# Two-layer trunk on one core: three query products of the second mixer placed among the latent norms and before the last head's rotation

## The chip, the cores and the metric

The kernel runs on one core of a Trainium2 chip. The metric is device time of the whole program in microseconds (us). The kernel before was run three times: 3219.42, 3215.95 and 3207.77 us, median 3215.95 us.

## The reference, cut to what matters

Two layers over 512 positions of width 1024, all in f32. Of one layer:

```
h = rmsnorm(x) * (1 + sc1) + sh1
proj = h @ w_in                      # xa_q 256, xa_kv 160, xb, xc, xd, gates 4*1024
y_a = mla_mixer(xa_q, xa_kv, ...)    # A: latents cq (256) and ckv (128), each with its own rmsnorm,
                                     #    then q = cq @ w_q_up, k and v = ckv @ w_kv_up; rope on 32 of 96 rows
y_b = chunk_relbias_mixer(xb)        # B: q, k, v of 8 heads straight from proj
y_c = diff_mixer(xc)                 # C
y_d = swa_sink_mixer(xd)             # D
merged = sum over the four of sigmoid(gates) * (y @ w_branch)
x = x + g1 * (merged @ w_out)
...                                  # second half: shared expert and 64 routed experts, top 6
```

The six modulations (sc1, sh1, g1, ...) are products of a short vector with `ada_w`, 48 column tiles of 128 for each layer.

## The kernel before

**Products and jobs.** f32 matrix products are done as three products of split operands: a weight tile is split into `w_hi` and `w_lo`, an activation into `h_hi` and `h_lo`, and hi*hi, hi*lo and lo*hi are added in one PSUM bank. The projections of the first half of a layer are written as jobs (`Job`, `make_jobs` L100). A job of the input projection is 8 slices of the contraction times 3, that is 24 products of 128x512 (L690); a job of a branch projection (`o_hi`) is 12, a job of the query latents (`cq_hi`, 96 rows) 6, a job of the key and value latents (`ckv_hi`) 3. Jobs use two PSUM banks in turn, so a job waits until the output of the job two before it has been copied out (by ScalarE, `act_out` from L701, or VectorE, `dve_out`).

**Weights.** SyncE loads weight tiles of 128x1024 (512 KB) into a ring of three buffers `raw` (`load_tile` L593). ScalarE makes `w_hi` (`split_hi`, L616), VectorE `w_lo` (`split_lo`, L624), each into two buffers in turn. A `raw` buffer is loaded again only when both halves of its tile have been split. The split of a tile is an event at the first product of the tile ahead of it in the stream (`events_of`).

**Modulations in the same ring.** The 48 column tiles of `ada_w` that a later stage needs go through the same ring. `place_ada` (L82) hangs them behind jobs: it takes the jobs with weights of projB, gbA, projC, gbB, projD, gbC and gbD, the last job of each phase left out, and sets tile i behind job i * (number of jobs) // 48. VectorE works such a tile off in one pass of 128x1024 (L823) behind the output of the job that it hangs on, and its `raw` buffer is free only then.

**Order on TensorE, by layer.** The order is the order of the code (from L1412). First the spread of the root of the first norm; projA (cq tile 0, cq tile 1, ckv, krope); then for cq and then for ckv the norm: `pe_norm_sums` (L895, column sums of squares with a vector of ones), `dve_norm_mean` (L901), `pool_norm_root` (L906), `pe_norm_spread` (L913, the root spread over a bank), `dve_norm_apply` (L926) and `act_norm_apply` (L944). The squares come from ScalarE (L882) and VectorE (L884). The sums and the spread use the same PSUM bank MB. Then the rotation of the shared key rows (L1422); upA (8 key jobs, 4 value jobs, 8 query jobs, with the rotation of head h-1, L1427, behind the job of head h); and the rotation of the last head. Then attention A (scores L984, transposes L1038, output L1118), in whose 17 steps the 16 jobs of projB are spread as filling (`spread`), and behind it, with no attention beside it, the gate stage gbA: four groups of two gate jobs of 24 products and two branch jobs of 12. Attention B is filled with projC and followed by gbB, attention C is filled with projD, attention D with gbC and followed by gbD. ScalarE and VectorE carry the same order in their own blocks (`act_stream` L794, `dve_stream` L807).

**Memory.** Before, the latents (`cqf`, `ckvf`, their split halves) lie in the area that qB, kB and vB take later.

## Time and profile before

| | |
|---|---|
| runs | 3219.42, 3215.95, 3207.77 us |
| median | 3215.95 us |
| the profiled execution | 3210.36 us, span 3208.7 us |
| TensorE busy | 2916.7 us (91%), 13756 matmuls |
| VectorE busy | 2033.4 us (63%) |
| ScalarE busy | 1568.6 us (49%) |
| GpSimd busy | 611.6 us (19%) |
| mean granted TensorE clock | 0.943 |

The shares are averages over the whole span, and the two layers each have a first half (mixers) and a second half (experts). The change lies in the first halves, at 72 to 770 us in layer 0 and at the same places 1580 us later in layer 1. The granted clock is 1.00 at 2.4 GHz and 0.50 at 1.2 GHz; a value between them is a mean over a stretch.

### The profile page before, as it was taken

To read this page: it belongs to the slowest core of one execution; us is meant where nothing else is said; L and a number is where in the kernel's file an instruction comes from. 1 tells how busy PE (TensorE), PEld (TensorE's weight loads), DVE (VectorE), ACT (ScalarE), POOL (GpSimd) and SP (SyncE) were. 2 spreads that over 40 slices of the span, in tenths; PEclk is the share of its full clock that TensorE was granted. 3 is DMA by queue.
4 is the path that set the end of the run, shared out by engine and by line. 5 is a ranking of instruction groups with operands and counts; after the bars stand their busy time and mean duration, and the time that the engine had idled before them with its cause. 6 is when DMAs were issued, how large, how long until landed. Compare 5 with 4: busy or idle time off the path is not lost. (4 is left out here: it accounts for less than half of the span.)

```text
span 3208.7 us, 42356 instructions
## 1 busy us (share of the span) xinstructions
PE 2916.7 (91%) x13756; PEld 2217.9 (69%) x13756; DVE 2033.4 (63%) x2871; ACT 1568.6 (49%) x2422; POOL 611.6 (19%) x577
## 2 busy tenths in 40 slices
PE   5899998899879999999579999989998899999993
PEld 4577776677667777777456777756776677777773
DVE  4544446454468888888645444555545788888885
ACT  2342423432347777777233334243223677777770
POOL 0100000100133333333210000000003233333332
PEclk9899999999789999999669999999998899999995
DMA  7124332233469999999412243312324799999975
GB/s 227 55 86 144 105 131 79 84 111 119 154 242 362 364 368 370 359 360 351 192 52 73 92 144 111 131 60 86 129 100 192 289 367 358 362 371 365 357 260 207
DMA packets 119333, 671.67 MB, mean 209 GB/s; under 512 B 27468, under 2 KB 28876, under 8 KB 84204
## 3 DMA queue, kind: packets, MB, share of 16 engines
q1 hardware_dynamic: 85792, 605.91, 50.7%
q0 software_dynamic: 31456, 57.70, 5.5%
q10 hardware_dynamic: 1932, 6.16, 0.8%
q8 instruction: 78, 1.28, 0.2%
q14 instruction: 75, 0.61, 0.1%
HBM read 656.86 MB, written 55.02 MB: 222 GB/s over the span
## 5 line engine op out<-in xcount | busy, mean ns | idle before, releaser
L1831 DVE TENSOR_TENSOR ew_lo<-ew,e_hi 128x2048 fp32r<-128x2048 f32 x260 | 595.8, 2292 | 191.9 <-ACT e_hi L1689 191.7
L690 PE MATMUL bank<-h_hi,w_hi 128*128 128x512 f32 x1248 | 514.5, 412 | 50.9 <-DVE w_lo L624 19.3
L1689 ACT ACTIVATE e_hi<-ew 128x2048 fp32r<-128x2048 f32 x260 | 497.5, 1914 | 105.4 <-PE bank L1976 81.5
L624 DVE TENSOR_TENSOR w_lo<-raw,w_hi 128x1024 fp32r<-128x1024 f32 x198 | 242.7, 1226 | 439.4 <-ACT w_hi L616 439.2
L690 PE MATMUL bank<-h_hi,w_lo 128*128 128x512 f32 x1248 | 503.1, 403 | 0.0
L690 PE MATMUL bank<-h_lo,w_hi 128*128 128x512 f32 x1248 | 500.8, 401 | 0.0
L1976 PE MATMUL bank<-e_hi,x_hi 128*128 128x512 f32 x1040 | 419.7, 404 | 0.0
L1976 PE MATMUL bank<-ew_lo,x_hi 128*128 128x512 f32 x1040 | 408.7, 393 | 0.0
L1976 PE MATMUL bank<-e_hi,x_lo 128*128 128x512 f32 x1040 | 406.5, 391 | 0.0
L616 ACT ACTIVATE w_hi<-raw 128x1024 fp32r<-128x1024 f32 x198 | 208.2, 1052 | 283.6 <-DMA raw<-in_wmix 184.3
L1591 POOL DMA_INDIRECT y_d<-y,idx x128 | 219.1, 1712 | 624.1 <-issue 527.0
L690 PEld LDWEIGHTS bank<-h_hi,w_hi 128*128 128x128 f32 x1248 | 240.2, 192 | 136.9 <-issue 47.0
L690 PEld LDWEIGHTS bank<-h_hi,w_lo 128*128 128x128 f32 x1248 | 240.5, 193 | 65.2 <-issue 12.4
L690 PEld LDWEIGHTS bank<-h_lo,w_hi 128*128 128x128 f32 x1248 | 240.7, 193 | 56.9 <-issue 8.7
L1011 ACT ACTIVATE pr<-sn,negmax 128x256 f32<-128x256 f32 (+3 forms) x256 | 137.0, 536 | 227.6 <-DVE negmax L1002 227.3
L1996 PE MATMUL bank<-ew,actT 128*128 128x512 f32 x520 | 247.2, 598 | 0.0
L1557 POOL DMA_INDIRECT xg<-h_d,idx x128 | 193.2, 1509 | 215.4 <-issue 203.3
L1976 PEld LDWEIGHTS bank<-e_hi,x_lo 128*128 128x128 f32 x1040 | 195.9, 188 | 44.1
L1976 PEld LDWEIGHTS bank<-e_hi,x_hi 128*128 128x128 f32 x1040 | 196.6, 189 | 38.5
L1976 PEld LDWEIGHTS bank<-ew_lo,x_hi 128*128 128x128 f32 x1040 | 196.6, 189 | 37.1
L1952 PEld LDWEIGHTS bank<-cst,xg 128*128 128x128 f32 x1040 | 123.8, 144 | 96.1 <-issue 68.7
L1824 DVE TENSOR_TENSOR x_lo<-bank,x_hi 128x512 fp32r<-128x512 f32 x260 | 166.7, 682 | 18.5 <-ACT x_hi L1681 18.5
(289 smaller groups left out, 4454.1 us busy)
## 6 DMA issues: line engine op xcount, KB each, us to landing
ew<-in_wexp SPq DMA_DIRECT2D x130, 2048.0 KB, 9.7
raw<-in_wmix SPq DMA_DIRECT2D x297, 512.0 KB, 4.0
ew<-in_wexp SPq DMA_DIRECT2D x130, 1024.0 KB, 9.4
yt<-y_d SPq DMA_DIRECT2D x8, 3072.0 KB, 15.6
ada0a<-in_ada SPq DMA_DIRECT2D x2, 2048.0 KB, 13.5
ada0b<-in_ada SPq DMA_DIRECT2D x2, 2048.0 KB, 22.3
h_d<-htok ACTq DMA_DIRECT2D x8, 512.0 KB, 2.7
xg<-h_d,idx POOLq DMA_INDIRECT x130, 9.4
```

What stands on the lines that cost most here:

```text
L616: nc.scalar.activation(w_hi[q % SPLIT][:], raw[u % RAW][:], ACT.Copy).then_inc(hi_done, 1)
L624: nc.vector.tensor_tensor(w_lo[q % SPLIT][:], raw[u % RAW][:], w_hi[q % SPLIT][:].bitcast(F32), ALU.subtract).then_inc(lo_done, 1)
L690: ins = nc.tensor.matmul(out, lhs, rhs, start=start, stop=stop)
L1011: nc.scalar.activation(pr[u % 4][:, 0:mp.nk], sn[u % 2][:, 0:mp.nk], ACT.Exp, bias=negmax[:, u:u + 1], scale=-1.0, accum_out=psum_of[:, u: ...
L1557: nc.gpsimd.indirect_dma_start(out=xg[s][0:n, :], out_offset=None, in_=h2_d, in_offset=bass.IndirectOffsetOnAxis(ap=idx[j % 8][0:n, 0:1].b ...
L1591: nc.gpsimd.indirect_dma_start(out=y_d, out_offset=bass.IndirectOffsetOnAxis(ap=idx[j % 8][0:n, 1:2].bitcast(U32), axis=0), in_=y[j % 2][0 ...
L1689: nc.scalar.activation(e_hi[h][:], up_part(ew, j, h), ACT.Copy).then_inc(whi_done, 1)
L1824: nc.vector.tensor_tensor(x_lo[j % 2][:, 4 * b:4 * b + 4, :], TB[b][:].rearrange("p (k t) -> p k t", k=4), x_hi[j % 2][:, 4 * b:4 * b + 4, ...
L1831: nc.vector.tensor_tensor(up_part(ew_lo, j, h), up_part(ew, j, h), e_hi[h][:].bitcast(F32), ALU.subtract).then_inc(wlo_done, 1)
L1952: ins = nc.tensor.transpose(TB[b][:, k * P:(k + 1) * P], xg[s][:, (4 * b + k) * P:(4 * b + k + 1) * P], ident)
L1976: ins = nc.tensor.matmul(G[s % 2][:], a, w, start=(h, k, i) == (0, 0, 0), stop=(h, k, i) == (1, 3, 2))
L1996: ins = nc.tensor.matmul(bank[1][:], actT[s % 2][:, f, :], raw_w[:, f, S:D], start=f == 0, stop=f == 1)
```

## The change

Of the four query jobs of mixer B, two (`early`: query tiles 0 and 1) run among the latent norms and one (`late`: query tile 2) ahead of the last head's rotation; projB keeps query tile 3, the key and value jobs and the turns. The krope job runs behind the sums of cq. The sums of the norms go to the bank OB, cq in columns 0 to 3 and ckv in 4 to 7, and no longer to MB; the spread now waits for MB itself. The latents lie in the gate buffers and in the area of the attention's output, so that qB can be written while they are in use. projB has 13 jobs in place of 16, so that `place_ada` divides 48 tiles over 87 jobs and not 90, and sets them at other jobs.

```diff
--- before.py
+++ after.py
@@ -107,7 +107,10 @@
                 + [Job("VA", [("kvup",)], "vA", act="ckv", k=1, arg=t) for t in range(TC)]
                 + [Job("T", [("qup", h // 4)], "qA", act="cq", k=2, m=DQ, col=DQ * (h % 4), arg=h) for h in range(HA)])
     for br, c in (("B", C_B), ("C", C_C)):
-        j["proj" + br] = ([Job("T", tile(c + P * i), "q" + br, arg=i) for i in range(4)]
+        q = [Job("T", tile(c + P * i), "q" + br, arg=i) for i in range(4)]
+        if br == "B":
+            j["early"], j["late"], q = q[0:2], q[2:3], q[3:]
+        j["proj" + br] = (q
                           + [Job("T", tile(c + P * (4 + i)), "k" + br, arg=i) for i in range(4)]
                           + with_turns([Job("T", tile(c + P * (8 + i)), "vt", arg=4 * (br == "C") + i) for i in range(4)],
                                        [Job("turn", [], "v" + br, arg=i) for i in range(4)]))
@@ -128,7 +131,7 @@
     return j
 
 
-ORDER = ("projA", "upA", "projB", "gbA", "projC", "gbB", "projD", "gbC", "gbD", "out", "shared")
+ORDER = ("projA", "early", "upA", "late", "projB", "gbA", "projC", "gbB", "projD", "gbC", "gbD", "out", "shared")
 
 
 def tile_stream():
@@ -260,12 +263,13 @@
         qB = place("qB", [P, 4, S])
         kB = place("kB", [P, 4, S])
         vB = place("vB", [P, TC, BW])
-        cqf = place("cqf", [P, 2, S], at=r1)
-        ckvf = place("ckvf", [P, 1, S], at=r1 + 4096)
-        cq_hi = place("cq_hi", [P, 2, S], F32R, at=r1 + 6144)
-        cq_lo = place("cq_lo", [P, 2, S], F32R, at=r1 + 10240)
-        ckv_hi = place("ckv_hi", [P, 1, S], F32R, at=r1 + 14336)
-        ckv_lo = place("ckv_lo", [P, 1, S], F32R, at=r1 + 16384)
+        cqf = place("cqf", [P, 2, S], at=t_end["gt0"] - 4 * S)
+        ckvf = place("ckvf", [P, 1, S], at=t_end["o_hi"] - 16 * S)
+        cq_hi = place("cq_hi", [P, 2, S], F32R, at=t_end["ckvf"])
+        cq_lo = place("cq_lo", [P, 2, S], F32R, at=t_end["cq_hi"])
+        ckv_hi = place("ckv_hi", [P, 1, S], F32R, at=t_end["cq_lo"])
+        ckv_lo = place("ckv_lo", [P, 1, S], F32R, at=t_end["ckv_hi"])
+        assert t_end["ckv_lo"] <= t_end["o_lo"] and t_end["cqf"] == t_end["gt1"]
         qC = place("qC", [P, 4, S], at=r0)
         kC = place("kC", [P, 4, S], at=r0 + 8192)
         vC = place("vC", [P, TC, BW], at=r0 + 16384)
@@ -558,7 +562,7 @@
 
 
         m_use = {}
-        for key in ([("st", n) for n in ("x",)] + [("rb", "x"), ("st", "cq"), ("rb", "cq"), ("st", "ckv"), ("rb", "ckv"), ("kr", 0)]
+        for key in ([("st", n) for n in ("x",)] + [("rb", "x"), ("rb", "cq"), ("rb", "ckv"), ("kr", 0)]
                     + [("qr", h) for h in range(HA)] + [("ot", o) for o in range(16)] + [("st", "x2"), ("rb", "x2")]):
             m_use[key] = len(m_use)
 
@@ -584,6 +588,7 @@
         def wait_mb_full(eng, key):
             eng.wait_ge(m_full, m_full_no[key] + 1)
 
+        norm_stats = {"cq": OB[:, 0:TC], "ckv": OB[:, TC:2 * TC], "x2": MB[:, 0:TC]}
         norm_no = {"cq": 0, "ckv": 1, "x2": 2}
         sq_k0 = {"cq": 0, "ckv": 2, "x2": 3}
         norm_k = {"x": KD, "cq": 2, "ckv": 1, "x2": KD}
@@ -886,19 +891,21 @@
 
         def pe_norm_sums(pe, name):
 
-            wait_mb_free(pe, ("st", name))
             K = norm_k[name]
+            stats = norm_stats[name]
+            if ("st", name) in m_use:
+                wait_mb_free(pe, ("st", name))
             for k in range(K):
                 n = sq_k0[name] + k
                 pe.wait_ge(sq_ready[n % 2], n // 2 + 1)
                 for t in range(TC):
-                    ins = nc.tensor.matmul(MB[:, t:t + 1], square_buf(name, n)[:, t * P:(t + 1) * P], ones[:, 0:1],
+                    ins = nc.tensor.matmul(stats[:, t:t + 1], square_buf(name, n)[:, t * P:(t + 1) * P], ones[:, 0:1],
                                            start=(k == 0 and t == 0), stop=(k == K - 1), skip_group_check=True)
                 ins.then_inc(sq_used, 1)
 
         def dve_norm_mean(dve, name):
             dve.wait_ge(sq_used, sq_k0[name] + norm_k[name])
-            nc.vector.tensor_scalar(stat[:, 0:TC], MB[:, 0:TC], 1.0 / (norm_k[name] * P), EPS, ALU.mult,
+            nc.vector.tensor_scalar(stat[:, 0:TC], norm_stats[name][:, 0:TC], 1.0 / (norm_k[name] * P), EPS, ALU.mult,
                                     ALU.add).then_inc(ms_ready, 1)
 
         def pool_norm_root(pool, name):
@@ -909,6 +916,7 @@
 
             if name in norm_no:
                 pe.wait_ge(rstd_ready, norm_no[name] + 1)
+                wait_mb_free(pe, ("rb", name))
             for t in range(TC):
                 ins = nc.tensor.matmul(MB[:, t * P:(t + 1) * P], rstd[:, t:t + 1].broadcast_to([P, P]), ident,
                                        start=True, stop=True)
@@ -1333,12 +1341,14 @@
                     act_norm_apply(act, "x", mod[:, 0:KD], h_hi, [pr[0][:], pr[1][:]])
                     act.wait_ge(lam_ready, 2)
                     nc.scalar.activation(lamt[:, 2:4], lamt[:, 0:2], ACT.Exp).then_inc(lame, 1)
-                    act_stream(act, events_of(whole(jobs["projA"])))
+                    act_stream(act, events_of(whole(jobs["projA"][:3])))
                     norm_squares(act, "cq", cqf, ready=lambda e, k: wait_out_of(e, "cq", k))
+                    norm_squares(act, "ckv", ckvf, ready=lambda e, k: wait_out_of(e, "ckv", 0))
+                    act_stream(act, events_of(whole(jobs["projA"][3:])))
                     act_norm_apply(act, "cq", None, cq_hi, [pr[0][:], pr[1][:]])
-                    norm_squares(act, "ckv", ckvf, ready=lambda e, k: wait_out_of(e, "ckv", 0))
+                    act_stream(act, events_of(whole(jobs["early"][:1])))
                     act_norm_apply(act, "ckv", None, ckv_hi, [pr[0][:], pr[1][:]])
-                    act_stream(act, events_of(whole(jobs["upA"])))
+                    act_stream(act, events_of(whole(jobs["early"][1:] + jobs["upA"] + jobs["late"])))
                     for i, br in enumerate("ABCD"):
                         act_attention(act, br)
                         if br != "C":
@@ -1365,12 +1375,15 @@
                                                              accum_out=lamt[:, i:i + 1]).then_inc(lam_ready, 1)
                     nc.vector.tensor_tensor(lamt[:, 6:7], vec[:, V_SUB:V_SUB + 1], vec[:, V_OML:V_OML + 1], ALU.mult)
                     nc.vector.tensor_scalar(sinkt[:, 0:32], vec[:, V_SINK:V_SINK + 32], -1.0, None, ALU.mult)
-                    dve_stream(dve, events_of(whole(jobs["projA"])))
+                    dve_stream(dve, events_of(whole(jobs["projA"][:3])))
                     norm_squares(dve, "cq", cqf, ready=lambda e, k: wait_out_of(e, "cq", k))
                     dve_norm_mean(dve, "cq")
+                    dve_stream(dve, events_of(whole(jobs["projA"][3:])))
                     dve_norm_apply(dve, "cq", cqf, vec[:, V_GQ:V_GQ + 2], None, cq_hi, cq_lo, [pr[0][:], pr[1][:]])
                     dve_norm_mean(dve, "ckv")
+                    dve_stream(dve, events_of(whole(jobs["early"][:1])))
                     dve_norm_apply(dve, "ckv", ckvf, vec[:, V_GKV:V_GKV + 1], None, ckv_hi, ckv_lo, [pr[0][:], pr[1][:]])
+                    dve_stream(dve, events_of(whole(jobs["early"][1:])))
                     dve.wait_ge(lame, 1)
                     link(dve, nc.vector.tensor_tensor(lamt[:, 4:5], lamt[:, 3:4], lamt[:, 2:3], ALU.subtract))
                     link(dve, nc.vector.tensor_tensor(lamt[:, 5:6], lamt[:, 4:5], vec[:, V_LI:V_LI + 1], ALU.subtract))
@@ -1394,6 +1407,7 @@
                         dve_stream(dve, events_of([(j, 0, n_products(j))]))
                         if j.out == "qA" and j.arg:
                             rotate(j.arg - 1)
+                    dve_stream(dve, events_of(whole(jobs["late"])))
                     rotate(HA - 1)
                     dve.wait_ge(tabA_ready, 1)
                     for i, br in enumerate("ABCD"):
@@ -1412,11 +1426,18 @@
                 @block.tensor
                 def _(pe):
                     pe_norm_spread(pe, "x")
-                    for j in jobs["projA"]:
-                        pe_products(pe, j, 0, n_products(j))
-                    for name in ("cq", "ckv"):
-                        pe_norm_sums(pe, name)
-                        pe_norm_spread(pe, name)
+                    def products_of(js):
+                        for j in js:
+                            pe_products(pe, j, 0, n_products(j))
+
+                    products_of(jobs["projA"][:3])
+                    pe_norm_sums(pe, "cq")
+                    products_of(jobs["projA"][3:])
+                    pe_norm_spread(pe, "cq")
+                    pe_norm_sums(pe, "ckv")
+                    products_of(jobs["early"][:1])
+                    pe_norm_spread(pe, "ckv")
+                    products_of(jobs["early"][1:])
                     wait_out_of(pe, "krope")
                     wait_mb_free(pe, ("kr", 0))
                     nc.tensor.matmul(MB[R, :], prot, qraw[R, :], start=True, stop=True).then_inc(m_full, 1)
@@ -1430,6 +1451,7 @@
                         pe_products(pe, j, 0, n_products(j))
                         if j.out == "qA" and j.arg:
                             rotate(j.arg - 1)
+                    products_of(jobs["late"])
                     rotate(HA - 1)
                     for br in "ABCD":
                         pe_attention(pe, br)
```

The listings below show one engine's instructions in program order: `w_hi_70` is buffer number 70, and so on.

ScalarE around the latent norms of a layer, before:

```order
L715 ACTIVATE ckvf<-bank 128x512
L616 ACTIVATE w_hi_70<-raw_68 128x1024
L882 ACTIVATE sn_74<-cqf 128x512
L944 ACTIVATE cq_hi<-pr_76 128x512
L944 ACTIVATE cq_hi<-pr_77 128x512
L882 ACTIVATE sn_74<-ckvf 128x512
L944 ACTIVATE ckv_hi<-pr_76 128x512
L616 ACTIVATE w_hi_71<-raw_69 128x1024
L717 ACTIVATE kA<-bank 64x512 x8
```

The same place of the change:

```order
L720 ACTIVATE ckvf<-bank 128x512
L887 ACTIVATE sn_74<-cqf 128x512
L887 ACTIVATE sn_74<-ckvf 128x512
L621 ACTIVATE w_hi_70<-raw_68 128x1024
L952 ACTIVATE cq_hi<-pr_76 128x512
L952 ACTIVATE cq_hi<-pr_77 128x512
L621 ACTIVATE w_hi_71<-raw_69 128x1024
L727 ACTIVATE qB<-bank 128x512
L952 ACTIVATE ckv_hi<-pr_76 128x512
L621 ACTIVATE w_hi_70<-raw_67 128x1024
L727 ACTIVATE qB<-bank 128x512
L621 ACTIVATE w_hi_71<-raw_68 128x1024
```

Both squares now stand together ahead of the next weight split, and two copies of query tiles and two splits stand among the applications of the norms (L952) and behind them.

TensorE at the last head's rotation, before (L1427 is a rotation, L984 the scores of attention A):

```order
L690 MATMUL bank<-cq_hi,w_hi_70 96x512
L690 MATMUL bank<-cq_lo,w_hi_70 96x512
L690 MATMUL bank<-cq_hi,w_lo_72 96x512
L1427 MATMUL bank<-qA,cst 32x512 x2
L984 MATMUL bank<-kA,qA 128x128 x2
L984 MATMUL bank<-kA,qA 128x256 x2
L690 MATMUL bank<-h_hi,w_hi_71 128x512
```

The same place of the change:

```order
L695 MATMUL bank<-cq_hi,w_hi_70 96x512
L695 MATMUL bank<-cq_lo,w_hi_70 96x512
L695 MATMUL bank<-cq_hi,w_lo_72 96x512
L1448 MATMUL bank<-qA,cst 32x512
L695 MATMUL bank<-h_hi,w_hi_71 128x512
L695 MATMUL bank<-h_lo,w_hi_71 128x512
L695 MATMUL bank<-h_hi,w_lo_73 128x512
```

The two rotations that stood together are parted by the 24 products of query tile 2, of which the last three rows are the first; the second rotation and the scores follow them.

VectorE at the boundary of the third and the fourth group of the second gate stage gbB (L775 and L778 multiply the gate with the branch and add it to the sum, L823 is a modulation tile, L624 a weight split), before:

```order
L778 TENSOR_TENSOR merged<-merged,gt_84 128x512
L823 ISA raw_68,mod<-raw_68,cb,vec 128x1024
L823 ISA mod 128x1
L624 TENSOR_TENSOR w_lo_73<-raw_67,w_hi_71 128x1024
L624 TENSOR_TENSOR w_lo_72<-raw_69,w_hi_70 128x1024
```

The same place of the change:

```order
L783 TENSOR_TENSOR merged<-merged,gt_84 128x512
L828 ISA raw_67,mod<-raw_67,cb,vec 128x1024
L828 ISA mod 128x1
L629 TENSOR_TENSOR w_lo_73<-raw_67,w_hi_71 128x1024
L828 ISA raw_69,mod<-raw_69,cb,vec 128x1024
```

A second modulation tile now stands behind the first gate job of this group.

## Rows read from the trace of the kernel before

**Rows 1.** Windows: start:end, us, busy PE, PEld, DVE, ACT, POOL, granted clock, DMA share, GB/s.
```profile
78.50:95.70 17.20, 10.06 (x44) 7.61 (x42) 6.13 (x12) 3.36 (x5) 2.04 (x2) 0.56 0.00 2
95.70:107.70 12.00, 12.00 (x37) 7.92 (x36) 5.27 (x7) 4.73 (x8) 6.29 (x5) 0.77 0.21 56
133.20:246.40 113.20, 112.44 (x666) 86.17 (x664) 50.67 (x116) 46.83 (x106) 3.06 (x6) 0.99 0.26 91
246.40:317.10 70.70, 68.39 (x290) 54.93 (x288) 30.18 (x37) 17.73 (x22) 0.00 (x0) 0.98 0.39 138
695.00:769.50 74.50, 67.45 (x290) 53.52 (x288) 34.61 (x45) 22.15 (x29) 0.00 (x0) 1.00 0.40 137
1675.30:1686.40 11.10, 11.10 (x37) 6.93 (x36) 5.27 (x7) 4.74 (x8) 6.29 (x5) 0.87 0.22 61
```

**Rows 2.** Waits of TensorE in attention A (133.2 to 246.4): us, times, longest.
```profile
PE bank L690 <- ACT gt L734: 0.4, 1, 0.4
```

**Rows 3.** Timeline of TensorE, 17 products inside attention A: start us, us busy.
```profile
147.08 0.40 PE L690 MATMUL bank<-h_lo,w_hi 128*128 128x512 f32 x1
...
150.72 0.39 PE L690 MATMUL bank<-h_hi,w_lo 128*128 128x512 f32 x1
```

**Rows 4.** Timeline of TensorE, last two rotations and first scores; [idle before <- releaser].
```profile
126.00 1.04 PE L1427 MATMUL bank<-qA,cst 32*32 32x512 f32 x2
127.91 1.30 PE L1427 MATMUL bank<-qA,cst 32*32 32x512 f32 x2 [0.87 <-DVE qrot L1389]
129.14 1.22 PE L984 MATMUL bank<-kA,qA 96*128 96x128 f32 x4
```

**Rows 5.** Timeline of TensorE, norms of the latents, layer 0.
```profile
72.69 0.39 PE L690 MATMUL bank<-h_hi,w_lo 128*128 128x512 f32 x1
...
78.44 0.95 PE L895 MATMUL bank<-ones,sn 128*128 128x1 f32 x8
80.11 1.34 PE L895 MATMUL bank<-ones,sn 128*128 128x1 f32 x8 [0.72 <-DVE sn L884]
82.83 2.07 PE L913 MATMUL bank<-cst,rstd 128*128 128x128 f32 x8 [1.38 <-POOL rstd L906]
87.68 1.84 PE L895 MATMUL bank<-ones,sn 128*128 128x1 f32 x8 [2.77 <-ACT sn L882]
90.86 2.07 PE L913 MATMUL bank<-cst,rstd 128*128 128x128 f32 x8 [1.34 <-POOL rstd L906]
93.86 1.88 PE L1422 MATMUL bank<-qraw,cst 32*32 32x512 f32 x2 [0.93 <-DVE pr L926]
95.67 0.80 PE L690 MATMUL bank<-ckv_hi,w_hi 128*128 128x512 f32 x1
```

**Rows 6.** Timeline of TensorE, 11 of the first latent products.
```profile
96.27 0.63 PE L690 MATMUL bank<-ckv_lo,w_hi 128*128 128x512 f32 x1
...
100.54 0.63 PE L690 MATMUL bank<-ckv_hi,w_lo 128*128 128x512 f32 x1
```

**Rows 7.** Waits of TensorE in the first gate stage (246.4 to 317.1).
```profile
PE bank L690 <- DVE w_lo L624: 2.3, 1, 2.3
```

**Rows 8.** Timelines of VectorE, ScalarE, TensorE in that stage, one chain.
```profile
263.87 1.28 DVE L823 CUSTOM_DVE_ANT_0 raw<-raw,cb,vec 128x1024 f32<-128x1024 f32 x1
...
268.55 1.06 ACT L616 ACTIVATE w_hi<-raw 128x1024 fp32r<-128x1024 f32 x1 [7.86 <-DMA raw<-in_wmix]
...
269.64 1.23 DVE L624 TENSOR_TENSOR w_lo<-raw,w_hi 128x1024 fp32r<-128x1024 f32 x1 [4.48 <-ACT w_hi L616]
...
271.01 0.47 PE L690 MATMUL bank<-h_hi,w_hi 128*128 128x512 f32 x1 [2.31 <-DVE w_lo L624]
```

**Rows 9.** Waits of TensorE in the second gate stage (427.1 to 497.0).
```profile
PE bank L690 <- DVE w_lo L624: 2.1, 2, 1.9
```

**Rows 10.** Waits of TensorE in the last gate stage (695.0 to 769.5).
```profile
PE bank L690 <- DVE gt L775: 5.4, 3, 2.3
PE bank L690 <- DVE w_lo L624: 1.5, 1, 1.5
```

## Prediction

> **What bounds the kernel now.** I read the views in this order: the share of each engine, to see which is the candidate; then the windows of each stage that the change touches; then in each stage what TensorE waited for; and last the timeline of the two places where work is put in. The kernel as a whole is a TensorE kernel, busy for 91% of the span, but the stages differ. In attention A TensorE is busy for 112.44 of 113.20 us at a clock of 0.99, while VectorE works 50.67 and ScalarE 46.83 [rows 1], and its one listed wait for a copy is 0.4 us [rows 2]. What is taken out there comes off the time one for one. Among the latent norms it is the other way round: TensorE is busy for 10.06 of 17.20 us, and the clock granted there is 0.56 [rows 1]; a chain of small steps over three engines sets the length. In the gate stages TensorE is bound again, but for some stalls on the ring of weight tiles and on VectorE: one of 2.3 us in gbA [rows 7], 2.1 in gbB [rows 9], 5.4 and 1.5 in gbD [rows 10]. So the change takes work from a stage that pays for it in full and puts most of it into a stage with idle time. All terms below are for one layer, and there are two.
>
> **1. Three query tiles leave attention A.** That is 3 x 24 = 72 products. Seventeen of them in a row start from 147.08 to 150.72, 3.64 us over 16 steps, so 0.2275 us each at the full clock [rows 3]. 72 x 0.2275 = 16.4 us. The other engines have room for the shorter steps: VectorE and ScalarE would still be busy for about half of 97 us [rows 1], and they lose copies and splits as well. **-16.4.** If steps of the attention began to wait for the softmax, part of this would stay; with cover of two to one I take the whole.
>
> **2. One query tile before the last rotation.** +24 x 0.2275 = +5.5 us. It stands where the second rotation waited 0.87 us for VectorE to finish the one before [rows 4]; that wait is covered now. **+4.6.** Its split and copy lie on ScalarE and VectorE beside 24 products that hide them. If the last rotation came late behind the split of the next tile on VectorE (1.23 us, [rows 8]), 0.4 more, which I leave out.
>
> **3. The latent norms.** Before, from the end of the products of ckv (72.69 plus 0.39, 73.1) to the first latent product at 95.67 it took 22.6 us [rows 5]. That held the 24 products of krope (5.5 us) and then sums, roots and spreads almost one behind the other. After, the chain on TensorE is: a wait for the copy and the square of the last cq tile, estimated at 1.2 from the two sums of cq (a wait of 0.72 and what the first sum leaves); sums of cq 0.95 + 1.34; krope 5.5, which hides the root; spread 1.0 to 2.07; sums of ckv 0.9 to 1.84; qB0 5.5, which hides the root and the application of cq; spread of ckv 1.0 to 2.07; qB1 5.5, which hides the application of ckv and the split of the latent weights; rotation 1.0 to 1.88. The upper values are the rows' own [rows 5], at a clock near one half; the lower are half of them, for the full clock. The sum is 23.9 to 27.9; I take 25.5, since the stretch now has three blocks of 24 products and should see the full clock for most of it. That is +2.9 for 48 products more, whose bare price is 10.9: the idle time of the norms takes in the rest.
>
> Behind it, the key and value products took 12.00 us at a clock of 0.77 in layer 0 and 11.10 at 0.87 in layer 1 [rows 1]. Eleven products at the low clock, from 96.27 to 100.54 in ten steps, are 0.427 us apart [rows 6], against 0.2275. If TensorE comes out of qB1 at the full clock, 36 products cost about 10, so 1 to 2 us come back; I take 1.5. Together **+1.4**, bounds -1 and +5.
>
> **4. The modulation tiles move.** With 87 jobs and not 90, projB loses two tiles (7 to 5), gbA and gbB each gain one (8 to 9), and in all gate stages they hang on other jobs. What such a tile costs is one chain [rows 8]: VectorE ends it at 265.15 (263.87 + 1.28), its buffer is loaded and the split begins at 268.55, 3.4 us later, the low half begins at 269.64, and the first product runs at 271.01, 5.86 us after the tile was done. A job of 24 products covers 5.5, so when the tile hangs on the second branch job and a second one on the next gate job, the following gate job stalls: 2.31 here. In gbA the new list has no such place but two groups that look like the groups of gbD, which stalls on VectorE's sum three times for 5.4 in all [rows 10]; since in gbA that sum is one pass, not two, I take 1 (0 to 4.6, gbD's 6.9 less the 2.3 it has). In gbB the last group has just that place, with one VectorE pass more ahead of it (estimate 2.3 + 0.7 to 1.2, so 3.5), and two boundaries like those of gbD that cost 2.3 and less, 3.1 together: 6.6 for 2.1 now, +4.5. In gbC and gbD one of the boundaries goes: -1.5. Sum **+4**, bounds -1 and +7. Attention B, C and D have the same number of tiles or nearly so, at zero.
>
> **5. Buffers and bank.** The latents in other buffers and the sums in another bank add no instruction. The new bank lets the sums of ckv be written while the spread of cq is still being read; that is in the sum of part 3. Two weight tiles more are needed among the norms; the DMA share there is 0.00 with the ring full [rows 1], so they cost nothing; uncovered, one would cost a load of 3.4 [rows 8].
>
> **Sum.** -16.4 + 4.6 + 1.4 + 4 = -6.4 for a layer, **-12.8** for two. From the profiled execution's 3210.4 that is 3197.6. That execution lies 5.6 below the median of the runs, 3215.95; against the median I forecast **3203 us**.
>
> **The rivals.** (R1) *The gate stages don't pay.* If the moved modulation tiles land in slack, part 4 falls to about -1 to 0 and part 3 to 0, and a layer gains 11 to 13 us: 3190 to 3195 in all. For it: TensorE's stalls in gbA and gbB are few now with nearly as many tiles [rows 7, 9]. Against it: the place that makes a stall of 2.31 is in the new list of gbB once, with more VectorE work ahead of it. Chance 0.30.
>
> (R2) *The moved products are given back almost whole.* Parts 3 and 4 at their bounds (+5 and +7) leave -16.4 + 4.6 + 12 = 0 a layer: 3210 to 3217. For it: gbD, whose pattern gbA and gbB take over, loses 6.9 us to such stalls in one stage [rows 10]. Against it: two bounds at once. Chance 0.15.
>
> (R3, slower) *The clock stays low.* Before, the norm stretch had a mean clock of 0.56 [rows 1] with TensorE busy for over half of it, and the first latent products ran 0.427 apart [rows 6]. If the bursts of 24 products between sums and spreads stay at 1.2 GHz, the 72 products of krope, qB0 and qB1 cost 0.2 us more each, +14.4 a layer, which with R2's part 4 is -6.4 - 4 + 14.4 + 7 = +11, so +22 in all: 3230 to 3240. It decides from some 32 of the 72 products at the low clock, where the gain of 6.4 is gone (6.4 / 0.2). Against it: in gbD four stalls of up to 2.3 us left the clock at 1.00 [rows 1, 10], and by part 3 no new gap is longer than those. For it: gbA with one such stall shows 0.98, not 1.00 [rows 1, 7]. Chance 0.07. The Trainium skill speaks for this rival (TensorE: Matmul & The Clock Gate, "A second HAM failure mode: psum-queue depth-cycling"): where TensorE idles briefly and often between groups of products, its clock swings between the two rates, and what is lost is the fall and the climb between bursts. By that rule the norm stretch would come out as in R3; gbD's row, four stalls at a clock of 1.00, doesn't bear it out for gaps of this size.
>
> That the change doesn't do what it says I give nothing: the listing shows the 24 products between the rotations. What is left, 0.03, is for things not thought of, on either side.
>
> **How the numbers follow.** The forecast with its own width, 3197 to 3210, has 0.45, R1 0.30, R2 0.15, R3 0.07. The range 3187 to 3214 takes in the forecast, R1 with its lower bounds and more than half of R2, over 0.8. About 0.5%, 16 us, is what a measurement of this kernel can tell from no change, so the border of faster is at 3200. R1 lies below it, and a quarter of the forecast's width: 0.30 + 0.12 = 0.42. Slower begins at 3232: 0.07. The rest is 0.51.
>
> **What would show it.** In the profile after: attention A shorter by 16 us with TensorE still busy for nearly all of it; 24 products between the last two rotations and no wait of 0.87 there; 24 to 28 us from the end of ckv to the first latent product, with a clock well over 0.56 and key and value products in about 10; TensorE's waits for w_lo and gt of 3 to 4 us in gbA, 6 to 7 in gbB, and one less in gbD. The prediction is wrong if attention A doesn't shorten by the full 72 products, if the norm stretch is longer than 28 us or shorter than 23, or if the waits in gbA and gbB stay at 2.3 and 2.1.

## The result and the profile after

The changed kernel takes 3191.03 us (median of 7 runs, 3178.43 to 3195.51). The kernel before has a median of 3209.29 us over seven runs, of which three stand ahead of the prediction with a median of 3215.95; 12.8 less than 3209.29 would have been 3196.5. The ratio is 0.9929 (0.9913 to 0.9945), a gain of 18 to 28 us, 23 in the middle (18 by the two medians). The forecast was 12.8 us less, most likely inside the 0.5% that count as no change; the time of 3191 lies inside the range of 3187 to 3214, but in the part given to the first rival. So the direction was right and the size about half of what came.

The profiled execution took 3187.87 us. Its first lines on the page:

```profile
span 3186.2 us, 42356 instructions
## 1 busy us (share of the span) xinstructions
PE 2903.4 (91%) x13756; PEld 2209.2 (69%) x13756; DVE 2033.6 (64%) x2871; ACT 1569.8 (49%) x2422; POOL 611.7 (19%) x577
```

The instructions are the same in number, so the 22.5 us between the two spans are waits and TensorE's clock (0.949 on the mean, 0.943 before). The windows of the stages after follow, with the columns of [rows 1]; the first is the norm stretch, then the key and value products, attention A, gbA, gbB, attention D with gbC, gbD, all of layer 0, and gbA of layer 1:

```profile
73.60:96.90 23.30, 22.11 (x115) 17.43 (x115) 9.03 (x14) 7.97 (x12) 2.04 (x2) 1.00 0.21 71
96.90:107.00 10.10, 9.96 (x38) 5.95 (x37) 5.31 (x8) 5.39 (x9) 6.29 (x5) 1.00 0.27 70
132.80:234.70 101.90, 98.64 (x602) 74.43 (x601) 47.86 (x116) 43.06 (x104) 3.06 (x6) 0.98 0.23 78
234.70:312.10 77.40, 70.57 (x292) 55.96 (x290) 30.97 (x39) 18.17 (x22) 0.00 (x0) 0.96 0.37 129
421.80:497.60 75.80, 68.86 (x290) 54.70 (x291) 35.85 (x47) 18.28 (x22) 0.00 (x0) 0.98 0.37 132
586.90:689.00 102.10, 100.80 (x586) 75.51 (x585) 59.31 (x144) 42.23 (x111) 5.16 (x11) 0.97 0.32 108
689.00:762.60 73.60, 67.40 (x290) 53.56 (x288) 34.75 (x45) 21.81 (x29) 0.00 (x0) 1.00 0.40 140
...
1801.80:1874.50 72.70, 67.62 (x290) 53.61 (x292) 30.88 (x40) 18.40 (x22) 0.00 (x0) 1.00 0.39 138
```

TensorE among the norms after, with the columns of [rows 5]. What stood in [rows 5] as six small operations with five gaps of 0.7 to 2.8 us is now small operations between blocks of 24 products, and one gap is left, the 1.21 ahead of the first sums. The sums of ckv take 0.95 us where they took 1.84, and a spread takes 1.05 where it took 2.07:

```profile
74.79 1.95 PE L902 MATMUL bank<-ones,sn 128*128 128x1 f32 x16 [1.21 <-ACT sn L887]
82.18 1.06 PE L921 MATMUL bank<-cst,rstd 128*128 128x128 f32 x8
83.07 0.95 PE L902 MATMUL bank<-ones,sn 128*128 128x1 f32 x8
89.45 1.05 PE L921 MATMUL bank<-cst,rstd 128*128 128x128 f32 x8
95.91 1.04 PE L1443 MATMUL bank<-qraw,cst 32*32 32x512 f32 x2
96.88 0.50 PE L695 MATMUL bank<-ckv_hi,w_hi 128*128 128x512 f32 x1
```

And ahead of attention A, with the columns of [rows 4]: query tile 2 fills the place between the last two rotations, and the wait of 0.87 is gone.

```profile
125.21 1.04 PE L1448 MATMUL bank<-qA,cst 32*32 32x512 f32 x2
126.18 0.50 PE L695 MATMUL bank<-h_hi,w_hi 128*128 128x512 f32 x1
...
131.86 1.04 PE L1448 MATMUL bank<-qA,cst 32*32 32x512 f32 x2
132.83 0.71 PE L992 MATMUL bank<-kA,qA 96*128 96x128 f32 x4
```

TensorE's waits in gbA (234.7 to 312.1), gbB (421.8 to 497.6) and gbD (689.0 to 762.6) after, two lines for each, to set beside [rows 7, 9, 10]:

```profile
PE bank L695 <- DVE merged L780: 4.1, 2, 2.1
PE bank L695 <- DVE w_lo L629: 2.7, 2, 2.0
...
PE bank L695 <- DVE w_lo L629: 4.6, 2, 3.3
PE bank L695 <- DVE gt L780: 2.3, 2, 1.6
...
PE bank L695 <- DVE gt L780: 3.9, 2, 2.3
PE bank L695 <- DVE w_lo L629: 2.3, 2, 1.7
```

The stages in us, layer 0 and layer 1, between the two profiles; the forecast is the one for a layer. An attention stage goes from the start of its first to the end of its last instruction on TensorE, and a gate stage is what lies between two of them (gbD ends with its own last product):

| stage | before | after | difference | forecast |
|---|---|---|---|---|
| norms: end of ckv to first latent product | 22.6, 22.3 | 23.3, 23.3 | +0.7, +1.0 | +2.9 |
| key and value products | 12.1, 11.1 | 10.1, 10.1 | -2.0, -1.0 | -1.5 |
| queries, rotations, query tile 2 | 21.4, 21.1 | 25.9, 25.9 | +4.5, +4.8 | +4.6 |
| attention A | 117.3, 118.3 | 101.9, 101.9 | -15.4, -16.4 | -16.4 |
| gbA | 70.6, 69.3 | 77.3, 72.6 | +6.7, +3.3 | +1 |
| attention B | 110.1, 109.7 | 109.7, 109.7 | -0.4, 0.0 | 0 |
| gbB | 69.6, 70.8 | 75.7, 75.8 | +6.2, +5.0 | +4.5 |
| attention C | 90.3, 91.8 | 89.4, 92.3 | -0.9, +0.6 | 0 |
| attention D with gbC | 108.1, 108.8 | 102.2, 102.9 | -5.9, -5.9 | gbC and gbD |
| gbD | 74.6, 74.9 | 73.6, 72.8 | -1.0, -2.1 | together -1.5 |
| sum | | | -7.5, -10.8 | -6.4 |

The stages give 18.3 of the 22.5 us. Of the other 4.2, most lies in the second half of layer 0, which the change doesn't touch (853.5 to 849.6).

The 77.3 of gbA in layer 0 belongs to this one execution. Runs 3 and 4 below have the same tiles at the same jobs of the gate stages, and there gbA takes 71.4 to 73.2.

### The profile page after: what moved, and what is told of

Its sections match the earlier page's. It is cut to its first block and busy times, and to the rows that moved or that the text cites. A ratio compares the mean times of both kernels' runs of the same rounds, so it can differ in the third digit from the quotient of the medians.

```text
span 3186.2 us, 42356 instructions
## 1 busy us (share of the span) xinstructions
PE 2903.4 (91%) x13756; PEld 2209.2 (69%) x13756; DVE 2033.6 (64%) x2871; ACT 1569.8 (49%) x2422; POOL 611.7 (19%) x577
## 5 line engine op out<-in xcount | busy, mean ns | idle before, releaser
L695 PE MATMUL bank<-h_hi,w_hi 128*128 128x512 f32 x1248 | 514.9, 413 | 56.3 <-DVE w_lo L629 21.2
L695 PE MATMUL bank<-h_hi,w_lo 128*128 128x512 f32 x1248 | 505.5, 405 | 0.0
L695 PE MATMUL bank<-h_lo,w_hi 128*128 128x512 f32 x1248 | 504.5, 404 | 0.0
L695 PEld LDWEIGHTS bank<-h_hi,w_hi 128*128 128x128 f32 x1248 | 241.4, 193 | 143.6 <-issue 49.4
L695 PEld LDWEIGHTS bank<-h_hi,w_lo 128*128 128x128 f32 x1248 | 241.8, 194 | 66.3 <-issue 13.7
L695 PEld LDWEIGHTS bank<-h_lo,w_hi 128*128 128x128 f32 x1248 | 241.9, 194 | 57.1 <-issue 8.5
## 6 DMA issues: line engine op xcount, KB each, us to landing
ada0b<-in_ada SPq DMA_DIRECT2D x2, 2048.0 KB, 22.3
```

Of the source, the lines that this page charges most:

```text
L695: ins = nc.tensor.matmul(out, lhs, rhs, start=start, stop=stop)
```

## The experiments

Ten runs followed, one of them the kernel before once more. All ratios are to the kernel before, run in the same rounds. The kernels that set the modulation tiles by a table do it with a small function in place of `place_ada`, so their lines stand 14 later: L709 is L695 of the change, and in run 9 L704 is L690 of before. In the cuts of edits the tables stand as comments, the jobs of a phase numbered from 0; in a gate stage jobs 0, 1, 4, 5, 8, 9, 12 and 13 are gate jobs and the others branch jobs. Where a stage's length is given, it is for layers 0 and 1, worked out as in the table above. Medians of different rounds differ by what the kernel before does in them (3206 to 3209), so kernels of different rounds are better set side by side by their ratios.

**1. The tiles of the gate stages at their old places.**

```diff
-    place_ada([j[phase] for phase in ("projB", "gbA", "projC", "gbB", "projD", "gbC", "gbD")])
+    place_ada(j)    # projB 0 1 2 3 4 6 8, gbA 1 3 4 6 8 10 12 14, gbB 0 2 4 6 7 9 11 13, gbC gbD 0 1 3 5 7 9 11 13
```

> The change, but with the modulation tiles of the gate stages and of projC and projD at the places of before (8 in gbA, 8 in gbB); projB's seven hang on its first jobs. Theory P (it is the places and the number in each gate stage that moved the stage times): gbA back from 77.4 and 72.7 to about 70, gbB from 75.8 to about 70, attention D with gbC back from 102 to about 108, gbD from 73 to about 74.7; per layer -5 - 5.5 + 6 + 1.5 = -3, so about 6 us faster than the change in all. Rival Q (the stages got longer because TensorE arrives there earlier and waits for the ring, wherever the tiles hang): gbA and gbB stay at 73 to 77, total as the change within 2 us.

Measured: 3185.71 us, 0.9939 (0.9924 to 0.9954), not told apart from the change by the totals. The stages are: gbA 68.9 and 71.5, gbB 69.5 and 70.2, attention D 107.3 and 106.8, gbD 74.3 and 75.0. Theory P holds stage by stage, and each place has its own price: against this run the change lost 6.7 us in gbA and gbB of layer 1 (14.6 in layer 0, with the gbA of 77.3) and got 6.1 back in attention D and gbD (5.8 in layer 0). Rival Q falls. TensorE's waits in attention D show 3.5 of the 5 us that the old places of gbC cost there (576.5 to 683.8); in the change only the wait for `negmax` (the maximum that the softmax takes off) is there:

```profile
PE bank L709 <- DVE gt L794: 2.6, 2, 1.9
PE bank L1006 <- DVE negmax L1024: 1.3, 1, 1.3
PE bank L1060 <- DVE pt L1073: 0.9, 1, 0.9
```

**2. Most tiles in the attention phases.**

```diff
+    # projB 0 1 2 3 4 5 6 8 8 10, gbA 0 5 8 12, projC 0 1 2 3 4 5 6 8 9 11, gbB 0 5 8 12,
+    # projD 0 1 2 3 4, gbC 0 1 3 4 5 8 9 11 12 13, gbD 0 1 5 9 12
```

> The change, but 35 of the 48 modulation tiles hang in the four attention phases (projB 10, projC 10, projD 5, gbC 10) and only 4, 4 and 5 in gbA, gbB and gbD, behind gate jobs as far as possible. Theory P: a gate stage holds 288 products, 65.5 us at 0.2275, and its stalls go: gbA, gbB and gbD 66 to 68 each, 6 to 9 less in each, so 18 to 24 a layer and 35 to 48 in all faster than the change, if the attention phases keep their lengths (102, 110, 91, 102). Rival R (the ring of three buffers moves about one tile per 3.5 us and the tiles cost as much where they go): the attention phases get longer by 2 to 4 us for each five tiles, and the total gains under 15 us.

Measured: 3224.33 us, 1.0054 (1.0033 to 1.0074), slower than before by 0.5%, and 40 us slower than the change by the ratios (33 by the medians). The gate stages did as theory P has it: 66.2 to 66.9 us at a clock of 1.00, with waits of 0.4 us at most. The attention phases lost far more: 107.8 and 109.7 (A), 117 (B), 104 and 105 (C), 117 and 116 (D). Rival R has the direction but not the size: 13 tiles more would be 5 to 10 us a layer by it, and the four phases got 41 to 43 longer. The windows of gbA, attention C and attention D, and below them attention C of the change:

```profile
244.40:310.60 66.20, 66.20 (x290) 53.89 (x290) 25.54 (x29) 17.73 (x22) 0.00 (x0) 1.00 0.38 133
...
494.00:597.70 103.70, 77.61 (x349) 55.18 (x348) 57.23 (x166) 38.49 (x122) 5.59 (x8) 0.86 0.16 59
597.70:715.20 117.50, 108.31 (x586) 78.59 (x585) 61.30 (x148) 41.88 (x111) 5.21 (x11) 0.92 0.29 102
```

```profile
497.50:586.90 89.40, 72.06 (x351) 51.24 (x350) 54.71 (x162) 37.97 (x122) 5.62 (x8) 0.94 0.19 65
```

Attention C needed 54.7 us of VectorE in the change and 57.2 here, so the work itself is not the price. Of the 14.3 us that it got longer, 8.8 are idle time of TensorE (103.70 - 77.61 against 89.40 - 72.06) and 5.5 are nearly the same products at a lower clock, 0.86 and not 0.94. In this kernel's order a weight split or a modulation tile on VectorE stands ahead of the softmax steps that follow it, so a tile that isn't there holds them up. That reading rests on the waits alone; no run takes it apart. In attention A VectorE's waits for `w_hi`, that is for the tile ahead of it in the ring, add up to 17.6 us with five modulation tiles (the change), 28.2 with seven (run 1) and 41.8 with ten (this run), always in nine waits:

```profile
DVE w_lo L629 <- ACT w_hi L621: 17.6, 9, 4.7
```

```profile
DVE w_lo L643 <- ACT w_hi L635: 28.2, 9, 5.0
```

```profile
DVE w_lo L643 <- ACT w_hi L635: 41.8, 9, 5.7
```

With seven the attention still hides it (100.7 and 102.0 us), with ten it doesn't.

**3. The sums of the norms in the old bank.**

```diff
+ [("rb", "x"), ("st", "cq"), ("rb", "cq"), ("st", "ckv"), ("rb", "ckv"), ("kr", 0)]
- norm_stats = {"cq": OB[:, 0:TC], "ckv": OB[:, TC:2 * TC], "x2": MB[:, 0:TC]}
+ norm_stats = {"cq": MB[:, 0:TC], "ckv": MB[:, 0:TC], "x2": MB[:, 0:TC]}
```

> The change, but the sums of the norms in the bank MB again, so that the sums of ckv wait until VectorE has read the spread of cq. Theory N (the bank of its own keeps TensorE busy between the blocks): a wait of about 2.5 us ahead of the sums of ckv (1.0 for the spread to end and 1.4 for the two passes of VectorE), the norm stretch 23.3 to about 25.8, the granted clock still 1.0; 5 us slower in all. Rival C (the clock falls after such a gap): qB0 and what follows at 1.2 GHz for some us, the stretch 28 or more, 10 us or more slower in all.

Measured: 3191.31 us, 0.9952 (0.9936 to 0.9969). By the ratios that is 7 us above the change, with intervals that overlap. The norm stretch is 28.3 us in both layers, 5.0 above the change at a clock of 0.88; in the profile gbA hides most of it (72.0 and 71.5 where the change's profile had 77.3 and 72.6). Two groups of products run 0.43 apart, those of krope (77.89 to 80.45) and those of qB0 behind the new wait of 1.50:

```profile
77.89 0.63 PE L695 MATMUL bank<-h_hi,w_hi 128*96 128x512 f32 x1
...
80.45 0.63 PE L695 MATMUL bank<-h_hi,w_hi 128*96 128x512 f32 x1
...
86.07 1.05 PE L902 MATMUL bank<-ones,sn 128*128 128x1 f32 x8 [1.50 <-DVE pr L934]
...
88.04 0.63 PE L695 MATMUL bank<-h_lo,w_hi 128*128 128x512 f32 x1
88.47 0.63 PE L695 MATMUL bank<-h_hi,w_lo 128*128 128x512 f32 x1
```

The krope job stands ahead of the wait that the bank makes, and it costs 1.6 us more here (7.16 from its start to the spread, 5.58 in the change's profile); it does the same in run 6 and in three other stretches, all with the bank of its own. So that part isn't shown to be the bank's. What lies at and behind the new wait is 3.3: 1.7 from the spread to the sums, and 1.6 for qB0 at the low clock. The bank of its own is worth these 3.3 us a layer, between the 2.5 of theory N and rival C, whose clock came but whose 10 us in all did not. I had set it at nothing, as part of the chain.

**4. Query tile 2 stays in attention A.**

```diff
-            j["early"], j["late"], q = q[0:2], q[2:3], q[3:]
+            j["early"], j["late"], q = q[0:2], [], q[2:]
```

> The change without the move of query tile 2: it stays in attention A's filling, the modulation tiles at the same jobs as in the change. Prediction's step 2 by the row of before: 5.5 us less ahead of attention A, the wait of 0.9 back, attention A longer by 24 products, 5.5; so 0.9 us a layer slower than the change, 1.8 in all. Rival: attention A's steps are now short enough to wait for the softmax, and filling of 24 products more costs less than 5.5 there: same as the change or faster by up to 4 us.

Measured: 3186.85 us, 0.9943 (0.9926 to 0.996), no difference from the change that can be told. By stages, the place ahead of attention A is 4.5 and 4.8 shorter, attention A 4.3 and 5.4 longer (106.2 and 107.3). The move of the third tile is worth -0.2 and +0.6 a layer, nothing that either theory could be told by.

**5. A mixed table.**

```diff
+    # projB 0 1 2 3 4 6 8, gbA, projC, gbB as before; projD, gbC, gbD as in the change
```

> The change with a mixed table of modulation tiles: projB, gbA, projC and gbB at the places of before (7, 8, 6, 8), projD, gbC and gbD at those of the change (3, 8, 8). Theory P (each place has its own cost): gbA and gbB about 70 as with the old places, attention D with gbC about 102 and gbD about 73 as in the change; 5 to 7 a layer less than with the old places everywhere, so 10 to 13 us faster than that kernel and 14 to 18 faster than the change. Rival Q2 (the places only pass the lateness on: what gbB saves, attention D loses): attention D back at 107, total as with the old places within 3 us.

Measured: 3171.13 us, 0.9889 (0.9875 to 0.9904), by the ratios 16 below run 1 and 13 below the change (15 and 20 by the medians). gbA 70.7 and 69.8, gbB 70.7 and 70.3, attention D 102.9 and 102.9, gbD 72.9 and 73.6. Theory P; lateness isn't passed on from stage to stage.

**6. No query product moved, the rest of the change kept.**

```diff
-            j["early"], j["late"], q = q[0:2], q[2:3], q[3:]
+            j["early"], j["late"], q = [], [], q    # and the tiles at the places of before
```

> All 16 jobs in projB as before and the table of before; of the change only the krope job behind the sums of cq, the bank of its own and the other buffers. Theory K (the krope job alone hides the first root): from the end of ckv's products to the first latent product 1.2 + 1.9 + 5.5 + 1.5 + 1.4 + a root of 1.4 + 1.5 + 0.9 + 1.8 = 17.1 (16 to 19) in place of 22.6, at a clock near 0.6; attention A 117 to 118, all other stages as before; so 5.5 a layer and 11 in all faster than before, half of what the change gains, without a query product moved. Rival (the query products make the gain): the stretch stays at 21 to 23 and the total within 3 us of before.

Measured: 3203.23 us, 0.9991 (0.998 to 1.0002), as before. The norm stretch is 20.1 us in both layers, 2.2 to 2.5 below before and 3.0 above what theory K needs; of the 3.0, 1.6 are products of the krope job at the low clock. The krope job does hide the first root, but the second is then bare, with a wait of 3.26, and the spread behind it is at the low clock again:

```profile
83.37 1.05 PE L935 MATMUL bank<-cst,rstd 128*128 128x128 f32 x8
84.26 0.95 PE L916 MATMUL bank<-ones,sn 128*128 128x1 f32 x8
88.47 2.07 PE L935 MATMUL bank<-cst,rstd 128*128 128x128 f32 x8 [3.26 <-POOL rstd L927]
```

With the two query tiles in, the stretch is 23.3: 48 products whose bare price is 10.9 cost 3.2 there (the change's profile has the krope job at the full clock, which is 1.6 of that in its favour), and 1.6 of it comes back in the key and value products (11.8 to 10.1). The theory fell; the gain needs the query products.

**7. The kernel before once more.**

> The kernel before once more, for a second profile of it. If the 4 us by which the second half of layer 0 differs between the two profiles is scatter of single executions, this profile has it 2 us or more away from the 853.5 of the first one; if it belongs to the change, it has 853 again.

One profile, 3207.12 us: the second half of layer 0 takes 852.5. By what was set down, that is not scatter of before. But runs 5 and 6 decide it: run 5, with the moved products, has 853.2, and run 6, without them, 848.7. Over all profiles it is 848.1 to 853.5 with either kind of kernel, and layer 1 has no such difference (857.6 before, 858.3 after). It doesn't follow the change, so the 4 us are a matter of single executions.

**8. Eight tiles behind the gate jobs, none behind a branch job.**

```diff
+    # as the mixed table, and gbA, gbB and gbD each 0 1 4 5 8 9 12 13
```

> As the mixed table, but the eight tiles of each of gbA, gbB and gbD hang behind the eight gate jobs, none behind a branch job. Theory G (a tile behind a branch job waits on VectorE for that job's sum, one behind a gate job doesn't): the gate stages 66 to 69, 2 to 4 less in each, 6 to 10 a layer faster than the mixed table. Rival R (twenty tiles through three buffers set the length): gate stages at 69 to 74 as they are, or longer where two modulation tiles stand in a row ahead of a branch tile.

Measured: 3141.26 us, 0.9803 (0.9789 to 0.9817): 63 us below before by the ratio, the lowest time here, with run 10 next to it. gbA 67.1 and 67.0, gbB 67.2 and 66.5, gbD 67.3 and 67.0: 13 a layer below run 5 in these three stages, more than the 6 to 10 that were set down. Theory G; three buffers do carry twenty tiles in such a stage. The windows of gbA and gbB show TensorE busy for all but 0.5 to 0.6 us. The DMA share is up from 0.37 to 0.44, and most of that is the shorter stage (129 GB/s over 77.4 us are 10.0 MB, 156 over 67.1 are 10.5). TensorE's one listed wait in gbA stands below them:

```profile
235.00:302.10 67.10, 66.49 (x290) 53.86 (x288) 30.30 (x37) 18.18 (x22) 0.00 (x0) 1.00 0.44 156
412.00:479.20 67.20, 66.69 (x290) 53.74 (x288) 35.07 (x44) 18.20 (x22) 0.00 (x0) 1.00 0.43 155
```

```profile
PE bank L709 <- DVE w_lo L643: 0.6, 1, 0.6
```

On VectorE the reason can be read. In the first group of gbA in run 5, the tile behind a branch job (L842) starts after that job's sum, which waits for TensorE; in run 8 both tiles of the group stand right behind a weight split, with no wait between:

```profile
252.28 0.69 DVE L794 SCALAR_TENSOR_TENSOR merged<-gt,bank 128x512 f32<-128x512 f32 x1 [0.65 <-PE bank L709]
252.89 1.28 DVE L842 CUSTOM_DVE_ANT_0 raw<-raw,cb,vec 128x1024 f32<-128x1024 f32 x1
```

```profile
245.44 1.23 DVE L643 TENSOR_TENSOR w_lo<-raw,w_hi 128x1024 fp32r<-128x1024 f32 x1 [4.94 <-ACT w_hi L635]
246.58 1.28 DVE L842 CUSTOM_DVE_ANT_0 raw<-raw,cb,vec 128x1024 f32<-128x1024 f32 x1
```

The stage starts at 235.4 in run 5 and at 235.0 in run 8, so the group's second tile starts 17.5 us into it there and 11.6 here, and its buffer comes free 6 us sooner.

**9. The kernel before with the table of run 8.**

```diff
-    place_ada([j[phase] for phase in ("projB", "gbA", "projC", "gbB", "projD", "gbC", "gbD")])
+    place_ada(j)    # as run 8, projB 0 1 3 5 7 9 13
```

> The kernel before, no query product moved, with the table of the run with eight gate jobs (projB's seven at their places of before). With the same tiles at the same jobs of the gate stages, what is left between the two is the moved products alone. By the stages of the profiles: norms 22.5 to 23.3, key and value products 11.6 to 10.1, queries and rotations 21.1 to 25.9, attention A 118 to 102, that is 0.8 - 1.5 + 4.8 - 16 = -11.9 a layer. Theory M (the moved products are worth 12 a layer, the tiles' shift took a part of it back in the change): this kernel at 3164 to 3168, some 38 below before by its tiles and 23 to 25 above the run with the moved products. Rival (the moved products are worth only the 18 to 20 that the change showed, and the good places do more where TensorE arrives earlier): 3159 to 3161, 18 to 20 above that run.

Measured: 3167.56 us, 0.9869 (0.9849 to 0.9889). Between this and run 8 only the moved products and what belongs to them are left. By the medians they are worth 26 us, by the ratios 0.66% or 21 us. By the four stages that they touch, 173.6 to 161.5 us in layer 0 and 172.7 to 161.2 in layer 1, so 12.1 + 11.5 = 23.6. Theory M (23 to 25) is nearer by the medians and the stages; the 21 of the ratios lies between it and the rival (18 to 20), and their intervals let in both. So it is the stages that decide.

**10. The tiles of gbC behind its gate jobs as well.**

```diff
+    # as run 8, and gbC 0 1 4 5 8 9 12 13
```

> As the run with eight gate jobs, and the eight tiles of gbC, which fill attention D, behind its gate jobs as well. Theory G: a tile behind a branch job waits for that job's sum there too: attention D 102 to about 98 to 100, 5 us faster in all. Rival (attention D is held by TensorE, busy 100.9 of 102.2 us in the change): the same within 2 us.

Measured: 3147.27 us, 0.9816 (0.9796 to 0.9836), not told apart from run 8. Attention D takes 104.1 and 103.9, 1 to 2 longer than in run 8. Theory G doesn't reach into a stage where the jobs are filling; there TensorE is busy for all but 1 to 3 us already.

## Why the prediction was right and wrong

**Step 1** (72 products out of attention A, -16.4): right, -15.4 and -16.4. TensorE's busy time there fell with the products, from 115.23 to 98.64 us in layer 0; the window in [rows 1] leaves out the first 4 us, and the whole stage before is

```profile
129.14:246.40 117.26, 115.23 (x673) 88.39 (x672) 53.45 (x123) 47.70 (x110) 3.06 (x6) 0.97 0.25 88
```

The softmax did not become the bound, though TensorE's listed waits rose from 2.0 to 3.2 us, the longest of them, for `negmax`, from 1.3 to 1.8.

**Step 2** (query tile 2, +4.6): right, +4.5 and +4.8, and run 4 shows that against the 24 products that it saves this is worth nothing.

**Step 3** (norms and key and value products, +1.4): the mechanism is right and the size was off; measured -1.3 and 0.0. The stretch was set at 25.5 and came to 23.3, below the lower end of the sum. The terms that failed are the spreads, the sums and the rotation, taken between their rows and the half of these: they came at the half, since the clock was 1.00 all the way, and the key and value products came at the full clock, too. The sums of cq were put at 2.29 by their rows of before and took 1.81 in one block. Run 3 shows how near the low clock is: one wait of 1.50 more costs 3.3. It also shows that the bank, which I gave no price, is one of the things that keep the gain.

**Step 4** (the modulation tiles, +4): the sum, +4.7 and +0.8, is near the forecast in one layer and below it in the other, but its parts were wrong. Attention D with gbC was put at nothing, on the ground that it has the same number of tiles; it gave 5.9 in both layers, and run 1 takes 4 to 5 of them back by the places alone. gbA was put at +1 and measured +6.7 and +3.3; its new groups stall on VectorE's sum as those of gbD do, though the sum there is one pass. The 6.7 is one execution's, and all profiles together say it better (old places: before and runs 1, 6 and 7; the change's: the change and runs 3 and 4; run 5 has the old ones in gbA and gbB and the change's in the other two):

| stage, both layers | old places | the change's places | between the medians | forecast |
|---|---|---|---|---|
| gbA | 68.9 to 71.5 | 71.4 to 77.3 | +2.0 | +1 |
| gbB | 69.5 to 71.4 | 73.7 to 76.6 | +5.5 | +4.5 |
| attention D with gbC | 106.1 to 108.9 | 101.6 to 102.9 | -5.2 | gbC and gbD |
| gbD | 74.3 to 75.0 | 72.5 to 74.1 | -1.8 | together -1.5 |

That is +0.5 a layer where I had +4. The prices of gbA, gbB and gbD were near, and gbB's waits in layer 0, too (6.9 where I had 6.6); the term at nothing for attention D is what failed. The number of tiles in a phase was the wrong thing to count. What counts in a gate stage is which job each hangs on: runs 8 and 9 have gate stages of 67 us with eight tiles where the old and the new places had 69 to 77. That doesn't explain attention D: there the old places have three tiles behind branch jobs and the change's cheaper ones have four, and run 10 with none is 1 to 2 us longer. Nor does it give the price of a single place, since gbD has three behind branch jobs with either list and differs by 1.8.

**Step 5** (buffers and bank, nothing): the tiles that were wanted early were there, TensorE waits for no weights in the norm stretch; the bank is dealt with above.

**Sum and chances.** -7.5 and -10.8 for the two layers in place of -6.4 each. Of the difference, -1.1 and -4.4, step 3 makes -2.7 and -1.4, and step 4 +0.7 and -3.2; in layer 0 the gbA of 77.3 hides what attention D gave. So two steps failed: step 3 by the size of its small operations, 2.2 us less than I took, and step 4 by the term at nothing for attention D, which measured -5.9. Without the tiles' shift, the moved products are worth 12 a layer by the stages (run 9); with the +0.5 of the places over all profiles that is 11.4, twice that 23, as the ratio has it. None of the signs that I had set for being wrong came clearly (attention A is 1.0 short of the 72 products in one layer, the stretch lies at 23.3, the waits in gbA and gbB rose to 6.8 and 6.9), and none of them looked at attention D. The first rival had the time right (3190 to 3195), and half by luck: part 3 was nil or below, as it said, but part 4 came near nothing because attention D gave back what the gate stages paid, and not because the tiles landed in slack. I gave it 0.30 and the side of faster 0.42, because the forecast lay 3 us short of the border. The third rival did not come with its 14 us a layer: its clock is seen in run 3, and in layer 0 of runs 1 and 2, where the stretch is 26.5 us at 0.87. Of the 14 norm stretches of the seven kernels that have both tiles there and the bank, nine are at 23.3, three at 24.9 and two at 26.5, and in all five the time is lost ahead of the first spread. The rule of the Trainium skill that spoke for it (TensorE: Matmul & The Clock Gate, "A second HAM failure mode: psum-queue depth-cycling"), a clock that falls and climbs between groups of products, fits these five, though behind one wait of 1.2 us and not many, and as a matter of 1.6 to 3.2 us; in the change's own profile the row has 1.00.

**Open.** Why gbC's places of the change are 5 us cheaper in attention D isn't known; runs 1 and 5 show that it is the places, and run 1's waits account for 3.5 of it. Why the same stretch holds the full clock in most executions and not in all wasn't settled. In the change's profile, 4 of the 22.5 us between the two spans lie in stretches that the change doesn't touch, and run 7 and the runs beside it put them down to single executions.

## What to carry to other kernels

Independent products put into a chain of small steps cost a third of their price here (3.2 of 10.9 us), if they are cut so that one block lies over each wait, and if no buffer makes the next step wait for the last; one wait of 1.5 us left in it cost 3.3. When an edit changes the length of a list that a formula spreads other work over, work out the new places and price each by what stands ahead of it in its queue, not by how many there are: here that moved single stages by 2 to 6 us either way, and placing it on purpose (run 9, 42 us by the ratio) was worth about twice the change itself. Work that waits for a transfer, put into a queue that also serves the critical chain, seems to cost that chain the wait and not the work (run 2, read from waits).

## What the runs showed of the hardware that I had not expected

The clock falls after less than I took from the rows of before, and not always. In run 3 the products of krope, behind one wait of 1.30 and 16 short products, start 0.43 apart from 77.89 to 80.45, and in run 6, behind a wait of 1.20, from 77.74 to 80.30, while the change's profile has a wait of 1.21 at the same place and 1.00 throughout. And gbD, before, kept 1.00 through four waits of up to 2.3 [rows 1, 10], while gbA after fell to 0.96 in layer 0 with four waits of up to 2.1 (6.8 in all) and held 1.00 in layer 1 with five of up to 1.6 (5.1 in all). The waits differ by 1.7 and the stages by 4.7; the other 3 are the clock's, since a mean of 0.96 over 77.4 us is about 6 us at the low level, where the work takes twice as long (a spread 2.07 us and not 1.05).
